# Eight-layer fp32 transformer on one core: per-step waits in the output projections, weights split two units ahead across the seams of the gated layers

## What is computed

```python
LAYERS = ("nsa", "ffn", "swa", "ffn", "even", "mlp", "odd", "mlp")
# attention-like: nsa (16 heads, compressed + selected + window), swa (16 heads, window and sinks),
#   even (8 heads, window, plus pooling), odd (8 heads, dense latent attention, plus a recurrent block)
out = o.reshape(b, s, N_HEADS * HEAD_DIM) @ w_out            # every attention layer ends so
def conv_ffn(h, w_in, conv_w, conv_b, w_out):                # "ffn", the gated layer, d_ff = 2816
    u = h @ w_in
    ...                                                      # c: causal convolution of u, three taps
    a, gate_in = jnp.split(c, 2, axis=-1)
    return (jax.nn.silu(a) * gate_in) @ w_out
def sq_relu_mlp(h, w1, w2):                                  # "mlp", d_ff = 4096
    u = jax.nn.relu(h @ w1)
    return (u * u) @ w2
```

## Time and profile before

| | us |
|---|---|
| median of three runs | 2379.38 |
| lowest and highest | 2373.97 and 2382.96 |
| the profiled execution | 2371.46 |
| its span, first to last instruction | 2369.3 |

### The profile page before, as it was taken

The page is one execution under the profiler, slowest core; times in us unless marked ns, Lnnn a source line. Parts: engine busy times, 40 slices in busy tenths (PEclk is TensorE's granted clock), DMA queues, the critical chain, the costliest instruction groups (busy, mean ns, idle before and its releaser), DMA issues.

```text
span 2369.3 us, 31700 instructions
## 1 busy us (share of the span) xinstructions
PE 2288.3 (97%) x12256; PEld 1827.6 (77%) x12256; DVE 1287.0 (54%) x1690; ACT 954.2 (40%) x1401; POOL 446.0 (19%) x431
## 2 busy tenths in 40 slices
PE   9998999999999889999999989999999999999998
PEld 7775678888888668888888668888888757888887
DVE  6447756664546666665547854333346685333333
ACT  4328843442324553443324453322224872322222
POOL 0003442110005134110004144200122004211010
PEclk9999999999999999999999999999999999999999
DMA  5211002222222112222223112322222201222231
GB/s 189 107 72 37 2 35 88 92 93 102 89 98 106 37 55 89 90 105 89 105 91 127 60 60 84 106 89 106 95 100 98 89 19 72 93 103 89 106 105 73
DMA packets 31499, 203.88 MB, mean 86 GB/s; under 512 B 4260, under 2 KB 5288, under 8 KB 7720
## 3 DMA queue, kind: packets, MB, share of 16 engines
q1 hardware_dynamic: 30104, 199.37, 23.4%
q10 hardware_dynamic: 1296, 3.15, 0.4%
HBM read 200.41 MB, written 2.10 MB: 85 GB/s over the span
## 4 chain that ended last, share of the span: by engine, by line
PE 84%; DVE 6%; ACT 6%; issue 2%; POOL 0%; DMA 0%; POOLq 0%; ACTq 0%; SPq 0%; DVEq 0%
PE D L593 75%; ACT prob L1344 2%; PE X L704 2%; PE D L730 2%; PE D L721 1%; DVE w_lo L1684 1%; ACT prob_t L1136 1%; ACT w_hi L1136 1%; DVE prob L2020 1%; PE X L833 1%; PE X L710 0%; PE X L659 0%; DVE xg L1712 0%; ACT mid L1136 0%; DVE conv_out L1838 0%
## 5 line engine op out<-in xcount | busy, mean ns | idle before, releaser
L593 PE MATMUL D<-xg,w_hi 128*128 128x512 f32 x3184 | 988.9, 392 | 4.7 <-DVE w_lo L1684 2.5
L593 PE MATMUL D<-mid,w_hi 128*128 128x512 f32 x2308 | 714.0, 391 | 16.8 <-DVE mid L1684 7.0
L593 PEld LDWEIGHTS D<-xg,w_hi 128*128 128x128 f32 x3184 | 598.4, 188 | 133.7 <-issue 5.9
L593 PE MATMUL D<-xg,w_lo 128*128 128x512 f32 x1592 | 621.3, 390 | 0.0
L1684 DVE TENSOR_TENSOR w_lo<-w_raw,w_hi 128x2048 fp32r<-128x2048 f32 (+2 forms) x210 | 459.6, 2190 | 288.6 <-ACT w_hi L1136 288.3
L1136 ACT ACTIVATE w_hi<-w_raw 128x2048 fp32r<-128x2048 f32 (+2 forms) x210 | 356.1, 1696 | 594.6 <-PE D L593 589.9
L593 PEld LDWEIGHTS D<-mid,w_hi 128*128 128x128 f32 x2308 | 433.0, 188 | 111.3 <-issue 12.0
L593 PE MATMUL D<-mid,w_lo 128*128 128x512 f32 x1154 | 449.6, 390 | 0.0
L593 PEld LDWEIGHTS D<-xg,w_lo 128*128 128x128 f32 x1592 | 299.8, 188 | 62.9
L1746 DVE TENSOR_TENSOR h<-D,h 128x1024 f32 (+1 forms) x71 | 86.9, 1224 | 352.8 <-PE D L593 352.7
L593 PEld LDWEIGHTS D<-mid,w_lo 128*128 128x128 f32 x1154 | 217.0, 188 | 45.2
(11 more groups left out here) (284 smaller groups left out, 1786.7 us busy)
## 6 DMA issues: line engine op xcount, KB each, us to landing
w_raw<-in_weights SPq DMA_DIRECT2D x184, 1024.0 KB, 4.8
h<-in_x SPq DMA_DIRECT2D x4, 512.0 KB, 7.4
out_y<-h SPq DMA_DIRECT2D x4, 512.0 KB, 2.9
w_raw<-in_weights SPq DMA_DIRECT2D x2, 512.0 KB, 7.1
inv_cnt<-in_inv_cnt ACTq DMA_DIRECT2D x1, 1024.0 KB, 5.0
cos<-in_cos ACTq DMA_DIRECT2D x3, 256.0 KB, 4.9
sin<-in_sin ACTq DMA_DIRECT2D x3, 256.0 KB, 5.3
vec<-in_vec SPq DMA_DIRECT2D x1, 272.0 KB, 2.8
```

Source lines behind the costliest of these rows:

```text
L593: last = nc.tensor.matmul(out, w[a], x[b], start=start and k == 0, stop=stop and k == 2)
```

## The change

Two edits that do not touch each other.

**Output projections of the four attention layers.** The wait for all tiles is gone. The first unit of the projection is written out anew: for its first output tile it goes through the input tiles in the order "those that are not of attention, then attention's in order", and only ahead of the last two, the seventh and the eighth product, does it wait for `ao_low` to count that tile. The four units stand one after another, with no loop.

**Gated layers.** Every unit, in every phase, is followed by the split of the unit two ahead: the last unit of an input phase now splits the second unit of the output phase behind it, ahead of its own taps. The tails are gone and the loops run one pass more. In the output phases VectorE adds the residual and then splits, where it split one unit ahead and then added.

```diff
-            def attention_ends(kind, l):
-
-                pe.wait_ge(ao_low, tiles_before[l] + TILES[kind])
-
-            def out_product(l, at):
-                with pe.Fori(0, 2) as i:
-                    for j in range(2):
-                        project(at["out"] + j, x_mid(0), i=i)
+            def out_product(kind, l, at):
+
+                u, tiles = at["out"], TILES[kind]
+                unit_arrives(u)
+                for o in range(2):
+                    for n, k in enumerate((*range(tiles, KD), *range(tiles))):
+                        if o == 0 and k in (tiles - 2, tiles - 1):
+                            pe.wait_ge(ao_low, tiles_before[l] + k + 1)
+                        last = product(D[:, 2 * (u % 2) + o, :], columns(u % 2, (o * KD + k) * P), x_mid(0)(k),
+                                       n == 0, n == KD - 1)
+                last.then_inc(w_used, 1)
+                project(u + 1, x_mid(0))
+                for j in range(2, 4):
+                    project(u + j, x_mid(0))
...
-                if layers[l] not in TILES:
+                if layers[l] == "mlp":
                     split_high(u0 + 1)
...
-                                if not isinstance(i, int) or k + 2 <= count:
-                                    split_high(u0 + k + 2, i)
+                                split_high(u0 + k + 2, i)
...
-                        if kind == "ffn":
-                            tail = 2
-                            if name != "in0":
-                                split_high(u0 + 1)
...
+                        ahead = 2 if kind == "ffn" else 1
                         with act.Fori(0, 2) as i:
                             for j in range(2):
-                                split_high(u0 + j + 1, i)
+                                split_high(u0 + j + ahead, i)
...
-                if ahead:
-                    split_low(u + 2, i)
+                split_low(u + 2, i)
...
                             for j in range(2):
-                                split_low(u0 + j + 1, i)
+                                if kind == "mlp":
+                                    split_low(u0 + j + 1, i)
                                 residual(u0 + j, 2 * i + j, i)
+                                if kind == "ffn":
+                                    split_low(u0 + j + 2, i)
```

More of the change, by code:

```diff
@@ L980, in nsa @@
                 attend("nsa", l, at["v"])
-                attention_ends("nsa", l)
-                out_product(l, at)
+                out_product("nsa", l, at)
             def swa(l, at):
@@ L997, in swa @@
                 attend("swa", l, at["q_last"])
-                attention_ends("swa", l)
-                out_product(l, at)
+                out_product("swa", l, at)
             def even(l, at):
@@ L1022, in even @@
                 attend("even", l, at["q_last"])
-                attention_ends("even", l)
-                out_product(l, at)
+                out_product("even", l, at)
             def recurrent_gates(u, t0, pairs):
@@ L1113, in odd @@
                 pe.wait_ge(yd_low, 4)
-                attention_ends("odd", l)
-                out_product(l, at)
+                out_product("odd", l, at)
             programs = {"nsa": nsa, "swa": swa, "even": even, "odd": odd}
@@ L1822, in scale_block, with ffn_unit @@
                     nc.vector.scalar_tensor_tensor(h[:, k, :], h[:, k, :], vec[:, c:c + 1], sq[:, :], ALU.mult, ALU.mult)
-            def ffn_unit(l, u, n, m, tile, ahead, i=0):
+            def ffn_unit(l, u, n, m, tile, i=0):
                 par, s = n % 2, u % 2
@@ L1873, in unit @@
                                 ffn_unit(l, u0 + k, conv_before[l] + before + k, inner_before[l] + before + k,
-                                         before + k, not isinstance(i, int) or k + 2 <= count, i)
+                                         before + k, i)
                             else:
@@ L1878, in feed_forward @@
                         done, tail = 0, 0
[L1879 to L1882, removed]
                         if name == "in0":
```

## The result

| us | before | after |
|---|---|---|
| median of five runs each | 2375.59 | 2358.59 |
| lowest and highest | 2373.97 and 2382.96 | 2357.01 and 2358.86 |
| the profiled execution, its span, its mean granted clock | 2371.46, 2369.3, 0.991 | 2358.59, 2356.7, 0.989 |

The change makes the kernel faster by 17.0 us; the ratio is 0.9919, with a 95% interval from 0.9902 to 0.9935. Timed side by side on two more chips, the two kernels gave 0.9913 (0.9898 to 0.9928) and 0.9920 (0.9907 to 0.9932). The sign was right, but the time lies under the range of 2361 to 2375. Note the spread as well: 9 us in five runs before, under 2 after. The mean granted clock is the clock that TensorE was granted, averaged over the span, as a share of its full speed.

The account below looks back on a forecast made before the run. TensorE, with 84% of the time on the chain, was taken as the bound, so only its waits could be won. 7.0 (projections) + 4.5 (seams) = 11.5 us off the median 2379.4 gave 2367.9, range 2361 to 2375.

Parts of the forecast that it names:

- The mechanism of the waits: TensorE's waits ahead of the projections and at the gated seams vanish, 7.0 and 4.5 us, without reappearing elsewhere.
- the seam's steps: First gated seam: moved split through at 552.4, VectorE's gated work ends at 556.6, residual starts at 559.07.
- 7.0 + 4.5 = 11.5 us: Total gain: listed TensorE waits removed ahead of four projections plus those at four gated-layer seams.
- the second term: Gated layers: four seam waits for `w_lo`, 1.1 to 1.2 us each, 4.5 us in all, removed by splitting earlier.
- The first term: Ends of the four attention layers: TensorE's wait for `mid` ahead of the projection, 7.0 us in all, removed.
- If the wait brings the low stretch, the gain is 11.5 + 1.65: Rival, chance 0.20: removing the wait behind `swa` attention also removes a low-clock projection stretch; gain 13.2 us, time 2366.2.
- that execution lies 7.9 us under the median of the runs, and below all three: Remark on the profiled execution of before, 2371.46 us; the gain was therefore subtracted from the median, 2379.4.
- Against: the other three attention layers have the same wait, and no such stretch follows: Argument against a clock gain: of four attention layers with the wait, only `swa` showed a low-clock stretch behind it.
- The range's lower end: 2361 us: the forecast less 1.65 of clock and less 5 for the spread of runs.
- half coming back: Rival, chance 0.15: attention gain lost at the next norm (2374.9), or seam gain lost to delayed gated work (2372.4).
- nothing: Rival, chance 0.06: the waits are re-created at the same length one step on; time stays 2379.4.
- slower: Rival, chance 0.04: TensorE runs out of instructions in the projections' longer straight code; net 2.1 us slower, 2381.5.

Follow-up runs that it names:

- seams-only kernel: Kernel before with only the gated layers' new split order, projections as before: 2369.71 us against 2378.01, ratio 0.9961.
- The projection alone: Kernel before with only the projection edit (waits ahead of products seven and eight, no loop), gated layers as before: 2364.26 us against 2378.01, ratio 0.9943.
- the straight code alone: Kernel before with only the projection's loop written out as four units, wait for all tiles kept: 2374.49 us against 2378.01, ratio 0.9984.
- the wait put back: Changed kernel with one wait for all attention tiles again ahead of the projection: 2365.99 us; on another chip 2365.53 against the changed kernel's 2358.31.

## Why the prediction was wrong

- **The mechanism of the waits was right.** Both groups of waits are gone and not moved; the eighth product does not wait; the seam's steps came within 0.4 us of the times worked out; nothing became late in their place.
- **"7.0 + 4.5 = 11.5 us": the second term was mis-sized.** I took the listed idle time for what the wait costs. At the seams it measured some 1.47 each in the first gated layer and 1.40 in the second, 5.7 in all. The first term stood in `nsa`, the one end of attention where it was measured by itself.
- **"If the wait brings the low stretch, the gain is 11.5 + 1.65": this is the step that failed.** The sum put the clock at nothing. It was a rival at 0.20, priced from the one layer of a single execution, while that execution had the highest clock of its kind. Over all runs of before whose clock is known (52, among them the profiled one) the mean clock is 0.9880 and the mean span 2374.9; over 14 of the changed kernel 0.9902 and 2355.9. A straight line through the 52 falls by 1.69 us for each 0.001 of clock, so 0.0022 are 3.7 us (an estimate: the line joins runs of one kernel, it is no price of a stretch). That and 12.7 make 16.4 of the 19.0 between the means; the measured median difference of the result is 17.0.
- **The base was off as well.** The forecast subtracts from 2379.38, the median of three runs; with two more it was 2375.59. Of the 9.3 us between 2367.9 and the measured 2358.59, 3.8 are this, which no step of the working could have told, and 5.5 are gain that the sum lacks.
- **The sign that I had and did not use**: "that execution lies 7.9 us under the median of the runs, and below all three". Carrying the sum over to the median took for granted that what the slower runs had more of would stay. A part of it hung on the wait that was removed.
- **"Against: the other three attention layers have the same wait, and no such stretch follows"**: true of that execution only. In the seams-only kernel it follows in three of four.
- **The range's lower end** came from the forecast less 1.65 and a spread of 5. With 5.7 for the seams and the 1.65 in three layers it would have been 2367.9 - 1.2 - 5.0 - 5 = 2356.7, which the measured 2358.59 would have met.
- Of the other rivals, half coming back, nothing, and slower, none showed. Straight code cost no time and the loop's entry was worth 1.2 us inside the 7.0.

Open: some 2.6 us of the 19.0 are not accounted for one by one. The same estimate on the mean spans of the parts says where they lie. The seams alone come out: 8.6 us, of which 5.7 are waits and 2.7 clock, so the loops of ScalarE and VectorE, with the tails in them, give next to nothing of their own. The projection alone leaves 1.9 of its 13.8 (7.0 waits, 4.9 clock), the straight code alone 1.2 of its 3.9 (1.2 and 1.5).

In the changed kernel a line through the 14 runs falls by only 0.43 us per 0.001, though their clocks, recorded to 0.001, go only from 0.989 to 0.992. So the low stretches that are left may cost it less, as they would in attention, where TensorE also waits for others: 30 us at 0.77 instead of 1.00, 6.9 us of clock lost, cost 4.1 us there, while 8 us at 0.79 behind `swa`, 1.7 lost, cost 1.65. That is one pair of executions. Nor is it settled why the wait put back in the changed kernel lowers the clock less than in the kernel before.

## What to carry to other kernels

A profiled execution that is faster than all the timed runs can hide a cost: find out what the runs have more of, here time at the low clock, and ask whether the change touches what brings it. Before two traces are compared, see whether they agree up to the first place that the change touches; here they were 3.0 us apart. Price a gap in a stream of matmuls by the step from one product to the next across it, not by the listed idle time. And when independent work waits for the last of many inputs, start with the inputs that are there; when a preparation is late although its inputs are early, look at what stands ahead of it in its own engine's program.

## What the runs showed of the hardware that was not expected

Adding twelve useless matmuls to each of four waits made the kernel 4.5 us faster (2370.88 against 2375.41). A gap of 1.16 us between full-size matmuls cost 1.46, a gap of 1.7 behind short ones, at the end of `nsa`, no more than its length. And idle times as short as 1.5 to 1.8 us at the end of attention were followed, in some layers and executions and not in others, by a stretch of projection at a granted clock of 0.62 to 0.82.
